# Routing on raw transposes, an expert choice for each tile, one key job moved to the third quad, and the rotary key in column halves

## The reference, cut to what matters

```python
# mixer: the shared rotary key, 32 channels of the input projection
k_rot = rotary(k_pe, cos, sin)
# cross attention of a layer: its keys depend on the memory alone
k = (rms_norm(mem, norm_mem[l]) @ xa_wk[l])
# mixture of experts
t = rms_norm(h, norm_ffn[l])                              # 256 x 1024
grp_prob = softmax(t @ wg + bg)                           # 4 groups
p_g, g_idx = top_k(grp_prob, 1)
exp_logits = einsum('td,gde->tge', t, we) + be            # 4 groups of 8
w_top, e_top = top_k(softmax(exp_logits of the chosen group), 2)
w_top = w_top / sum(w_top) * p_g
for e in range(32):
    y = y + combine[:, e] * ((silu(t @ w_gate[e]) * (t @ w_up[e])) @ w_down[e])
h = h + y
```

## Time and profile before

| | us |
|---|---|
| three runs | 951.7, 953.39, 953.81 |
| median | 953.39 |
| the profiled execution: its own time | 951.7 |
| the profiled execution: span from first to last instruction | 949.6 |

### The profile page before, as it was taken

How to read it: one execution, slowest core, us unless ns; L and a number is a source line. 1 busy time by engine, 2 the same in 40 slices (tenths; PEclk the granted TensorE clock), 3 DMA queues, 4 the chain that set the end, 5 groups by cost and what they waited for, 6 DMA issues and landing times.

```text
span 949.6 us, 11933 instructions
## 1 busy us (share of the span) xinstructions
PE 856.2 (90%) x5052; PEld 562.5 (59%) x5052; DVE 331.5 (35%) x659; ACT 158.5 (17%) x377; POOL 15.0 (2%) x21
## 2 busy tenths in 40 slices
PE   7999999999999989887989999999996898877666
PEld 6888875699576435334627887668954543332321
DVE  2427475142243222212115756713223322221214
ACT  2101135312110000000012113531210100000002
POOL 0500000000000000000000000000000000000000
PEclk9999999999999999799999999999998899899898
...
GB/s 357 356 177 100 133 189 167 89 266 178 9 357 368 429 427 428 425 427 426 425 427 331 100 133 177 178 89 304 186 43 358 268 429 413 429 429 426 422 427 184
DMA packets 23499, 272.71 MB, mean 287 GB/s; under 512 B 2960, under 2 KB 3344, under 8 KB 5776
## 3 DMA queue, kind: packets, MB, share of 16 engines
...
HBM read 270.81 MB, written 1.05 MB: 286 GB/s over the span
## 4 chain that ended last, share of the span: by engine, by line
PE 69%; DMA 17%; PEld 5%; issue 4%; DVE 3%; ACT 1%; DVEq 0%; PEldq 0%; ACTq 0%
PE bank L514 17%; DMA ring<-in_expert_units 17%; PE bank L590 12%; PE bank L626 6%; PE bank L911 6%; PE bank L613 4%; PE bank L671 4%; PE bank L568 3%; PE bank L656 3%; PE bank L576 2%; PEld bank L613 2%; PE bank L943 2%; PE bank L924 1%; PE bank L733 1%; PEld bank L514 1%
## 5 line engine op out<-in xcount | busy, mean ns | idle before, releaser
L626 PE MATMUL bank<-ring,xT 128*32 128x512 f32 x944 | 122.1, 657 | 43.5 <-DMA ring<-in_expert_units 43.5
L514 PE MATMUL bank<-uT,ring 128*128 128x256 f32 (+1 forms) x512 | 114.2, 381 | 0.0
L626 PEld LDWEIGHTS bank<-ring,xT 128*32 128x32 f32 x944 | 30.1, 115 | 126.2 <-issue 83.5
L514 PEld LDWEIGHTS bank<-uT,ring 128*128 128x128 f32 (+1 forms) x512 | 94.5, 187 | 16.3 <-issue 0.7
L613 PE MATMUL bank<-sel,hn 128*128 128x128 f32 x512 | 66.3, 292 | 14.3 <-issue 12.3
L613 PEld LDWEIGHTS bank<-sel,hn 128*128 128x128 f32 x512 | 64.5, 208 | 16.6 <-issue 14.7
L671 PE MATMUL bank<-yy,turned 128*128 128x512 f32 x128 | 66.1, 640 | 4.5 <-DVE h L1860 4.5
L1846 DVE TENSOR_TENSOR hid<-hid,bank 128x256 f32<-128x256 f32 x16 | 6.7, 422 | 166.5 <-ACT hid L1300 166.5
L911 PEld LDWEIGHTS bank<-uT,ring 128*128 128x128 f32 x512 | 57.8, 192 | 1.1 <-DVE uT L1399 0.5
L911 PE MATMUL bank<-uT,ring 128*128 128x128 f32 x512 | 57.8, 275 | 0.0
L590 PE MATMUL bank<-ring,qT 128*128 128x512 f32 x128 | 56.3, 592 | 0.0
(11 more groups left out here) (290 smaller groups left out, 942.9 us busy)
## 6 DMA issues: line engine op xcount, KB each, us to landing
ring<-in_expert_units SPq DMA_DIRECT2D x87, 2048.0 KB, 19.0
ring<-in_fixed_units SPq DMA_DIRECT2D x16, 2048.0 KB, 7.7
...
early<-in_expert_units SPq DMA_DIRECT2D x9, 2048.0 KB, 7.7
...
```

What stands on the lines that cost most here:

```text
L514: mm = pe.matmul(o[row0:row0 + m], w[:, c, c0:c0 + m], rhs[:, c], start=(c == 0), stop=(c == chunks - 1))
L626: mm = pe.matmul(bank[2][32 * e:32 * e + 32, :], xT[:, 2 * n + c, 32 * e:32 * e + 32], w[:, e, :, c], start=(n == 0 and c == 0), stop=(n = ...
```

## The change

Six things change, most of them in both layers.

1. TensorE turns the rows of `h` itself, without waiting for the normalisation (`raw_transposes`); VectorE multiplies the logits with `rs` when it takes them out of the bank (`logits`). The weights and gains are packed in the order that fits, on the host. `hn`, which the gathers read, is now written by ScalarE and signalled by `normed`; the first gather waits for it.
2. The choice is made for each tile by itself (`choose(t)`, the same steps on one tile), each followed by its own count: `places0` of one matmul, `places1` of two, and `totals` of two for the number of rounds. `choose(0)` stands between jobs of tile 1.
3. TensorE's job `xout3` is cut in two (chunks 0 to 2, then 3 to 7), and `router1` too, with the transposes between the parts.
4. The softmax weights are started behind `sel` instead of inside the choice.
5. The key job `xk1` of the next layer moves from ahead of the first quad into the third (quad 2), and `xk0` is cut into pieces of 2, 10 and 4 matmuls (`part_of_keys`).
6. The eight matmuls of `kp` go alternately to the lower and the upper 64 output partitions; VectorE multiplies both halves, and `pe_sum` has ones for all 128 rows.

```diff
-NEXT_BEFORE_STEP, NEXT_IN_QUAD, NEXT_BEHIND_LAYER = ["xk0", "xk1"], {3: "xk2", 4: "xk3", 5: "xv0", 6: "xv1"}, ["xv2"]
+NEXT_BEFORE_STEP, NEXT_IN_QUAD, NEXT_BEHIND_LAYER = ["xk0"], {2: "xk1", 3: "xk2", 4: "xk3", 5: "xv0", 6: "xv1"}, ["xv2"]
...
-              ("xout1", "V", 6), ("xout2", "V", 7), ("ffn_xt0", "V", 0), ("ffn_xt1", "V", 1), ("xout3", "V", 2),
-              ("router0", "V", 3), ("ffn_xt2", "V", 0), ("ffn_xt3", "V", 1), ("router1", "V", 6)]
+              ("xout1", "V", 6), ("xout2", "V", 7), ("ffn_xt0", "V", 0), ("ffn_xt1", "V", 1), ("router0", "V", 3), ("ffn_xt2", "V", 0),
+              ("xout3", "V", 2), ("ffn_xt3", "V", 1), ("places0", "V", 7), ("router1", "V", 6)]
+PLACES = [("places1", "V", 5), ("totals", "V", 7)]
...
-JOBS += [(1, "xk0", "A", 4), (0, "places", "V", 7), (1, "xk1", "A", 5)]
+JOBS += [(0, *job) for job in PLACES] + [(1, "xk0", "A", 4)]
 JOBS += [(1, name, "A", 3) for name in NEXT_IN_QUAD.values()]
-JOBS += [(1, *job) for job in MIX_INPUTS + [("xv2", "A", 5)] + LAYER_JOBS[4:]] + [(1, "places", "V", 7)]
+JOBS += [(1, *job) for job in MIX_INPUTS + [("xv2", "A", 5)] + LAYER_JOBS[4:] + PLACES]
...
+            def part_of_keys(name, o, n0, n1):
+                w = slot_view(name, 1)
+                for n in range(n0, n1):
+                    k, c = n // KC, n % KC
+                    mm = pe.matmul(o[:, k * S:(k + 1) * S], w[:, c, k * P:(k + 1) * P], memN[:, c], start=(c == 0), stop=(c == KC - 1))
                 return mm
...
-                channel_tile(o[:, 0:S], w, P, 2 * ROPE, uT).then_inc(pe_job, 1)
+                for c in range(KC):
+                    rows = slice(2 * ROPE * (c % 2), 2 * ROPE * (c % 2) + 2 * ROPE)
+                    mm = pe.matmul(o[rows, 0:S], w[:, c, P:P + 2 * ROPE], uT[:, c], start=(c < 2), stop=(c >= KC - 2),
+                                   tile_position=(0, 2 * ROPE * (c % 2)))
+                mm.then_inc(pe_job, 1)
...
-                transposes("ffn", hn, 0)
+                def raw_transposes(t, n):
+                    wait_emptied(lay, f"xout{2 * t + n}")
+                    o = begin(f"ffn_xt{2 * t + n}")
+                    for c in range(4):
+                        mm = pe.transpose(o[:, c * P:c * P + P], h[:, t, (4 * n + c) * P:(4 * n + c + 1) * P], ident)
+                    mm.then_inc(pe_job, 1)
+                def router(o, t, n):
+                    after(f"ffn_xt{2 * t + n}")
+                    for c in range(4 * n, 4 * n + 4):
+                        mm = pe.matmul(o[:, 0:NG + NE], uT[:, c, t * P:t * P + P], w_rout[:, c], start=(c == 0), stop=(c == KC - 1))
+                    return mm
+                raw_transposes(0, 0)
+                raw_transposes(0, 1)
                 free_unit("xout2")
-                to_rows("xout", oT, base, 1, 1)
+                to_rows("xout", oT, base, 1, 1, range(3))
+                pe.wait_ge(M["params"], in_layer(lay, "params", 32))
+                o = begin("router0")
+                router(o, 0, 0)
+                router(o, 0, 1).then_inc(pe_job, 1)
+                raw_transposes(1, 0)
+                to_rows("xout", oT, base, 1, 1, range(3, KC))
+                r1 = begin("router1")
+                router(r1, 1, 0)
+                raw_transposes(1, 1)
                 free_unit("xout3")
-                pe.wait_ge(M["params"], in_layer(lay, "params", 32))
-                def router(t):
-                    after(f"ffn_xt{2 * t + 1}")
-                    o = begin(f"router{t}")
-                    for c in range(KC):
-                        mm = pe.matmul(o[:, 0:NG + NE], uT[:, c, t * P:t * P + P], w_rout[:, c], start=(c == 0), stop=(c == KC - 1))
-                    mm.then_inc(pe_job, 1)
-                router(0)
+                pe.wait_ge(M["r_chosen"], in_layer(lay, "r_chosen", 1))
+                pe.matmul(begin("places0")[:, 0:NE], tb("before"), chosen[:, 0], start=True, stop=True).then_inc(pe_job, 1)
                 if lay == 0:
                     pe.wait_ge(next_gained, 1)
                     wait_unit(base, "xk0", 1)
                     k0 = begin("xk0", 1)
-                    key_tile(1, "xk0", k0, 0, memN)
-                transposes("ffn", hn, 1)
-                router(1)
+                    part_of_keys("xk0", k0, 0, 2)
+                router(r1, 1, 1).then_inc(pe_job, 1)
                 if lay == 0:
-                    key_tile(1, "xk0", k0, 1, memN).then_inc(pe_job, 1)
-                    wait_unit(base, "xk1", 1)
-                    k1 = begin("xk1", 1)
-                    key_tile(1, "xk1", k1, 0, memN)
-                pe.wait_ge(M["r_chosen"], in_layer(lay, "r_chosen", 1))
-                o = begin("places")
-                both = chosen.rearrange("p t e -> p (t e)")
-                pe.matmul(o[:, 0:2 * NE], tb("before"), both, start=True, stop=True)
-                pe.matmul(o[:, 2 * NE:4 * NE], tb("ones"), both, start=True, stop=True).then_inc(pe_job, 1)
+                    part_of_keys("xk0", k0, 2, 12)
+                pe.wait_ge(M["r_chosen"], in_layer(lay, "r_chosen", 2))
+                o = begin("places1")
+                pe.matmul(o[:, 0:NE], tb("ones"), chosen[:, 0], start=True, stop=False)
+                pe.matmul(o[:, 0:NE], tb("before"), chosen[:, 1], start=False, stop=True).then_inc(pe_job, 1)
+                o = begin("totals")
+                pe.matmul(o[:, 0:NE], tb("ones"), chosen[:, 0], start=True, stop=False)
+                pe.matmul(o[:, 0:NE], tb("ones"), chosen[:, 1], start=False, stop=True).then_inc(pe_job, 1)
                 if lay == 0:
+                    part_of_keys("xk0", k0, 12, 2 * KC).then_inc(pe_job, 1)
                     free_unit("xk0", 1)
-                    key_tile(1, "xk1", k1, 1, memN).then_inc(pe_job, 1)
-                    free_unit("xk1", 1)
-                after("places")
+                pe.wait_ge(M["normed"], in_layer(lay, "normed", 6))
...
-                    junk = uT[:, 0:4].rearrange("p c s -> p (c s)") if t == 0 else squares
-                    sum_squares(h, junk, t, "xout")
+                    sum_squares(h, hn[:, t].rearrange("p c k -> p (c k)"), t, "xout")
                     first_rstd(4, t)
+                    act.wait_ge(M["ffn_rstd"], in_layer(lay, "ffn_rstd", t + 1))
+                    act.activation(hn[:, t].rearrange("p c k -> p (c k)"), h[:, t], ACT.Copy, scale=rs[:, t:t + 1]).then_inc(M["normed"], 1)
...
-                gone(dve.tensor_tensor(kpr[:, :], o[0:2 * ROPE, 0:S], ropeT[0:2 * ROPE, 1], ALU.mult))
+                for odd in range(2):
+                    rows = slice(2 * ROPE * odd, 2 * ROPE * odd + 2 * ROPE)
+                    st(dve.tensor_tensor(kpr[rows, :], o[rows, 0:S], ropeT[rows, 1 - odd], ALU.mult))
+                settle()
+                dve.sem_inc(dve_emptied, 1)
...
-                norm_and_add("xout", hn.rearrange("p t c k -> p t (c k)"), 4, "ffn", 3)
+                mean_square(4, 0)
+                refine(4, 0)
+                dve.sem_inc(M["ffn_rstd"], 1)
+                add_bank("xout", 1, 0)
+                keep_transposes("ffn", 3, 0)
...
+                def logits(t):
+                    o = job(f"router{t}")
+                    gone(dve.scalar_tensor_tensor(lg[:, t], o[:, 0:NG + NE], rs[:, t:t + 1], b_rout[:, :], ALU.mult, ALU.add))
+                    dve.wait_ge(dve_emptied, emptied(lay, f"router{t}"))
...
+                logits(0)
+                keep_transposes("ffn", 3, 1, (0,))
+                choose(0)
+                add_bank("xout", 1, 1)
+                keep_transposes("ffn", 3, 1, (1,))
+                put_places(0)
+                mean_square(4, 1)
+                refine(4, 1)
+                dve.sem_inc(M["ffn_rstd"], 1)
+                logits(1)
+                choose(1)
+                put_places(1)
...
+                st(dve.tensor_tensor(exp_g, gl, top_g.unsqueeze(2).broadcast_to([P, T, NG]), ALU.subtract))
+                st(dve.tensor_tensor(gap, top2, top1, ALU.subtract))
+                settle()
+                dve.sem_inc(M["r_exp"], 2)
+                gone(dve.tensor_reduce(rounds_f[:, :], job("totals")[:, 0:NE], AX.X, ALU.max))
```

115 lines of the change are left out of this document (44 added, 71 removed).

## The result

The changed kernel takes **938.67 us** (median of 4 runs, 936.06 to 940.02); the kernel before, on the same chip, 953.38 us (4 runs, 951.7 to 953.81). The ratio is 0.9848 with a 95% interval of 0.9833 to 0.9862, a gain of 14.7 us. I had 937.

The account below looks back on a forecast made before the run. The end was taken to move with each layer's first gather while the queue has a hole. 6.6 (first layer) + 5.8 (second) + 2 x 1.7 (rotary key) = 15.8 us off 951.7 gives 935.9, adjusted to 937; range 931 to 944.

Parts of the forecast that it names:

- What bounds the kernel: Both layers: the end moves with the first gather while the queue has a hole; at most 8.7 us in the second.
- Second layer, up to the gather: Second layer's routing, from xout3 to the first gather: gather 5.8 us earlier, passed on whole to the end.
- VectorE falls behind: Rival, chance 0.10: slower operations lengthen both choices by 1.3 us, costing 2.6 in the second layer; 941.5 us.
- a sign of being wrong: Routing, VectorE: choose(0) ending after xout3 would show the forecast wrong; it was expected at 724.4, xout3 at 724.6.
- First layer, up to the gather: First layer's routing with key matmuls between its steps: first gather 9.1 us earlier, mostly xk1's 16 matmuls, 6.9 us.
- First layer, the stream: First layer's expert queue up to unit e21: 1 MB more costs 2.45 us, so e21 lands 6.6 us earlier.
- The megabyte moved into quad 2: First layer, quad 2: xk1's fill ends at 340.0; e21, in its slot, could land 3.0 us ahead of need.
- no starved quad: Against the rival, chance 0.11, that quad 2's fill starves the queue: 940 us, or 944 with all 6.6 gone.
- The price of 2.45: First layer's stream: the 1 MB of xk1 moved into quad 2 takes 2.45 us of transfer.
- Rotary key: Both layers, kp: two halves run side by side, from 3.5 to 1.75 us, 1.7 us per layer.
- Clock: Rival, chance 0.10: TensorE at half speed through the first up or in the first layer, 2 to 4 us each; 941.
- The sum: Whole kernel: 6.6 + 5.8 + 2 x 1.7 = 15.8 us off the profiled 951.7, so 935.9.

Follow-up runs that it names:

- e8: The changed kernel run once more as it is, for its spread: 938.85 us.
- e9: Changed kernel with the first tile's choice placed behind the addition of xout3's second half and the last drain: 948.92 us.
- run e6: Changed kernel with the scaling of hn on VectorE in place of ScalarE: 939.84 us.
- e10: Changed kernel with the first layer's early unit, issued behind router1, issued later, behind the unit that waits for the gather: 941.38 us.
- e3: Changed kernel with xk1 back ahead of the first quad: 942.17 us.
- e1: Kernel before with the rotary key in column halves and nothing else: 947.67 us, ratio 0.9965.
- run e5: Kernel before with xk1 moved to quad 2 and nothing else: 951.49 us, ratio 0.9985.
- e21: Not a run: an expert unit of the first layer's stream, for which TensorE waits in quad 3; forecast to land at 351.6, 6.6 us earlier.
- e4: Changed kernel without xk1's transfer and matmuls, its keys copied from xk0's, so work is left out: 938.81 us.
- e11: Changed kernel without xk1's transfer and matmuls, its keys copied, timed a second time: 937.17 us.
- e2: Changed kernel with the rotary key as before, without the halves: 941.51 us.

## Why the prediction was right, and where its sum was off

- **What bounds the kernel** held. In the second layer the transposes came 6.1 us earlier (714.17 to 708.06), the gather 11.75 and e6's issue 12.26, and the span is 12.4 shorter: whatever the gather won there came through to the end. In e8 it was 14.3 at the gather and 13.3 at the end, so nearly all.
- **Second layer, up to the gather**: 5.6 measured, 5.8 forecast. Seen from `xout3`'s start the gather comes at 19.46 us (708.93 to 728.39), where I had 19.3. The second choice is 0.4 longer, and the steps ahead of it and behind it are 0.3 shorter. The Trainium skill, VectorE: DVE Perf Modes, section on the TRN2 errata, holds that each operation on SBUF pays a fixed latency; the trace agrees, since three steps on an eighth of the elements took 0.63 us against 0.73. The two rows from which I had argued for this, the bias addition and the copy, read a bank and not SBUF, so they did not bear on it. Half the width saved next to nothing; my 3.4 for the choice with its offset was 3.9, because it was a mean over pairs of operations that don't wait for each other.
- **VectorE falls behind** was a rival at 2.6 us and is real at 0.35, with 0.4 more in the second choice: `choose(0)` ends 0.35 behind `xout3`, which I had named as a sign of being wrong. e9 shows what it stands in front of, 10 us.
- **First layer, up to the gather**: 8.9 against 9.1.
- **First layer, the stream**: this is the term that was mis-sized. I wrote "e5 ... lands at 288.4 or 289; both are ahead of e6 and need nothing more". e5 did land there (issued at 279.58 with 9.3 to landing, 288.9), but e6 needs 4.9 us of queue behind it. Alone it would have landed at 285.48 + 7.7 = 293.2; behind e5 it is 293.8 at best, and it was 294.9. In e8 the same sum gives 293.3 (e5 landed at 288.4), and it was 295.0. The last 1.1 and 1.7 I can't resolve. They go with the early unit in front of e5: in the six traces that have the three in a row as close as changed has, e6 takes 9.2 to 10.0 us, in run e6, the seventh, 8.5; where the early unit is behind e6 (e10), or further ahead (e3, e9), it takes 7.5 to 7.9. The order of before gave 7.6 and once 9.0 (e1), and 7.7 with xk1 moved (run e5); the 9.0 stood behind a unit that landed at 296.2, 4.9 ahead of e6. e21 came 5.4 us earlier (358.2 to 352.8) where my sum, with the rotary key's 1.7, had 8.3. Of the 2.9 that lack, 0.55 are the gather's own (the transposes came 1.35 earlier, where the key's gain was to be 1.7) and about 1.8 e6's landing, with some 0.5 more on the queue behind it. By e8 only about 1 us of these 2.3 belongs to the kernel (two units behind e6, 1.0), which would have made the forecast 938.
- **The megabyte moved into quad 2**: no starved quad, as forecast. e21 takes the slot of xk1 and is issued at 339.48, where I had 340.9, 13.3 us ahead of its landing; alone it would have needed 7.7, and the rate stays between 418 and 438 GB/s from 296 to 348 us. The price of 2.45 was seen at e21 when the megabyte was taken out (e4, e11) and not in the time.
- **Rotary key**: 1.95 us in place of 3.7 in the rows, 2.8 to 3.5 us over both layers in time by e2 and 3.3 by e1's ratio. Right.
- **Clock**: the second layer's gather still runs at about half speed (5.38 against 3.81), the first `up` does not. No loss beyond what was there.

The sum gave 935.9 on the profiled execution of before; that of after took 940.02, 4.1 more. The first layer lacks 2.9 at e21 and 1.1 more by its end, where the clock took 2.2; 0.7 lie outside the span; the second layer gave back 0.6. The medians are 14.7 apart, against 15.8 by the sum. The interval of the gain, 13.2 to 15.9 us, holds 15.8, so the times alone don't show that the sum was off; the traces show the queue's part, about 1 us. And that 937 came so near owes something to errors of both signs, as with the choice, 0.4 longer, and the steps around it, 0.3 shorter. Nor does any run take back the transposes of `h`, the choice for each tile or the pieces of `xout3` one by one (e9 moves the first choice only); what each of them gives is argued from the timelines and not shown.
